# First attention: a unit's transposes and value products one step later, transposes ahead of the scores

## The chip, the core and the metric

The program runs on one core of one Trainium2 chip. The metric is the device time of that core in microseconds (us). The engines are called as the profile calls them: PE is TensorE (matrix products and transposes; PEld is its weight load), ACT is ScalarE, DVE is VectorE, POOL is GpSimd, SP issues most DMAs. Each engine works through a program of its own, in the order in which it is written; semaphores hold it until another engine has come far enough.

## The reference, cut to what matters

Two transformer blocks run one after the other on 512 tokens of width 1024, in float32. The change touches the attention of the first block only:

```
proj  = rmsnorm(x) @ w_in                       # q, k, v of all heads, gates
o_swa = softmax(q.k/8 - slope*dist, window 128, with a sink) @ v      # 8 heads, 2 kv heads
o_cmp = softmax(q.k_cmp/8 - slope*dist) @ v_cmp                       # 8 heads, 31 compressed keys
o_sl, o_win = softmax(q.k/8 - slope*dist, causal) @ v                 # 8 heads each
o_nsa = gate0*o_cmp + gate1*o_sl + gate2*o_win
x     = x + rmsnorm(concat(o_nsa, o_swa) @ w_o)
```

(The selection may keep 16 blocks and there are only 8, so `o_sl` is plain causal attention.) After it come a gated MLP with a convolution, an embedding, and the second block (neighbourhood attention, retention, MLP). None of that is touched.

## The kernel before, in words

**Number format.** Every float32 operand is held as a high part and a low part, and a product of two such operands takes three matmuls (`triple`, lines 593 to 595). ACT makes the high part of a weight piece (line 1323), DVE or, for pieces that come four after a fill piece, POOL makes the low part (lines 2022 and 2943).

**Units.** The first attention is cut into 28 units. Units 0 to 7 are "swa" (one head each, scores in two PSUM banks). Units 8 to 27 are four rounds of five: one "cmp" unit (both kv heads at once, one bank), then "sl", "wn", "sl", "wn" (one head each, three banks). A wide unit u passes through these stages:

1. PE: scores (`scores1`, lines 799 and 800), 8 matmuls.
2. DVE: bias added, row minimum taken, from PSUM to the buffer `pp` in SBUF (`soft1`, line 2191).
3. ACT: exponential and row sum, in place (line 1510).
4. DVE: reciprocal of the four row sums (`norm1`, line 2272). POOL: four multiplications of `pp` by the reciprocal, and by the gate (lines 2969 and 2971). The texts call this the division.
5. PE: transposes (`turn1`, line 813), 7 in a swa unit, 10 in another, into two or three banks. The first transposes of an sl or wn unit already need all four multiplications.
6. ACT: high part of the transposed probabilities (line 1516). DVE: low part, which also frees the banks (`rest1`, line 2207).
7. PE: value products (`values1`, lines 826 and 827), 8 matmuls; cmp units and the second sl unit of a round bring one matmul of line 866.
8. Where the unit closes an output (every swa and every wn unit): ACT copies half of it out (line 1521), DVE adds the other half (`out_add`, line 2214); for every second one ACT and DVE then split the pair (lines 1525 and 2219).

A cmp unit does the same with small tensors and with its division on DVE (lines 2260 to 2266).

**Steps.** All five engines run one loop over steps s, each with its own stages and its own order. In step s PE does: weight matmuls of a fill piece (12 matmuls for a piece; `FILL1`, line 29, says which pieces go into which step: projections, later the output product `w_o_swa`), scores of unit s+1, transposes of unit s-1, value products of unit s-2. DVE does: scaling of a filled product, `soft1(s)`, `out_add(s-3)`, the low part of a pair, reciprocal of s-1, `rest1(s-2)`, low parts of filled queries or keys. ACT does: copies of filled products (line 1533 is that of `w_o_swa`), exponential of s, high part of a weight piece, high part of transposed s-1, output half of s-2, high part of a pair. POOL does: division of s-1, low part of a weight piece.

**PSUM banks.** The eight banks are handed out first in, first out (`Banks`, line 178): who takes a bank waits until the readers of what it held before are done. Banks of scores of unit s and of transposes of unit s-2 are given back at the start of PE's step s.

**Buffers.** `pp` has three buffers, taken in turn by wide units; `soft1(u)` waits for the transposes of the wide unit three before. The transposed probabilities have two; ACT waits for the value products of the wide unit two before.

Of the kernel before, what the change touches and what calls it, by code (L numbers as in the profile page):

```python
# [27 lines left out]

FILL1 = {0: [("w_swa", 6), ("w_swa", 7)], 1: [("w_swa", 8)], 2: [("w_nsa", 0), ("w_swa", 9)], 3: [("w_nsa", 1)],
         4: [("w_nsa", 8)], 5: [("w_nsa", 9)], 6: [("w_nsa", 2)], 8: [("w_nsa", 3)], 9: [("w_nsa", 10)],  # L30
         10: [("w_nsa", 11)], 11: [("w_nsa", 12)], 12: [("w_o_swa", 0), ("w_nsa", 13)],
         14: [("w_o_swa", 1), ("w_o_swa", 2)], 15: [("w_nsa", 14)], 16: [("w_nsa", 15)], 18: [("w_o_swa", 3)],
         21: [("w_o_swa", 4)], 23: [("w_o_swa", 5)], 26: [("w_o_swa", 6)], 27: [("w_o_swa", 7)]}

# [217 lines left out]
def build(nc, ins, out):  # L252
    ctx = ExitStack()
    with ctx:
# [272 lines left out]
        def out_key(u):  # L527

            kind, j, g = unit(u)
            return ("ob", "swa" if kind == "swa" else "nsa", j, g)  # L530

        def closes(u):
            return unit(u)[0] in ("swa", "wn")
# [4 lines left out]
        def out_sum(key):  # L538
            return OS[key[2] % 2]
# [43 lines left out]
        def tensor(e):  # L583
# [188 lines left out]
            def comp_keys():  # L772
                b, free = bank.take(("kc",))
                e.wait_ge(*free, s_fn.at(("hid", 0)))
                t.matmul(b[0:64, 0:62], cw2[0][:, :], chid[0][:, 0:62], start=True, stop=True).then_inc(*s_cm.up("kc"))
                bank.give(("kc",))
# [103 lines left out]
            def give_turned(u):  # L880
                for i in range(1 if unit(u)[0] == "cmp" else 2 if unit(u)[0] == "swa" else 3):
                    bank.give(("tr", u, i))
# [6 lines left out]

            scores1(0)  # L890
            later = []
            for s in range(N_UNITS + 2):
                if s < N_UNITS:
                    give_scores(s)
                if s >= 2:
                    give_turned(s - 2)
                for name, i in FILL1.get(s, ()):
                    key, n = fill_info(name, i)
                    if name == "w_o_swa":
                        part(name, i, B, swa_out, [4, 5, 6, 7], key, True, True)  # L900
                    else:
                        part(name, i, A, x0s, [4 * n, 4 * n + 1, 4 * n + 2, 4 * n + 3], key, n == 0, n == 1,
                             (lambda j, kv=HIDDEN[name, i]: hidden_quarter(kv, j)) if (name, i) in HIDDEN else None)
                    if n == 1:
                        later.append(key)
                if s == 1:
                    comp_keys()
                if s + 1 < N_UNITS:
                    if s + 1 == 8:
                        comp_values()  # L910
                    scores1(s + 1)
                for key in later:
                    bank.give(key)
                later.clear()
                if 1 <= s <= N_UNITS:
                    turn1(s - 1)
                if s >= 2:
                    values1(s - 2)

            def nsa_out(k):  # L920
                return s_xl.at(("ob", "nsa", k))
# [388 lines left out]
        def scalar(e):  # L1310
# [207 lines left out]
            def out_part(key, g, dst, ready, *free):  # L1518

                e.wait_ge(ready, *free)  # L1520
                a.activation(dst[half(g), :], bank.ap(key)[half(1 - g), :], ACT.Copy).then_inc(*s_cp.up(key))
# [16 lines left out]
                    keys_of(key[1], KS1[key[1]])  # L1538

            later = []  # L1540
            for s in range(N_UNITS + 3):
                for name, i in later:
                    filled(name, i)
                if s < N_UNITS:
                    kind, j, g = unit(s)
                    if kind == "cmp":
                        e.wait_ge(s_sf.at(s))
                        for g in range(2):
                            p3 = pc[:, :].rearrange("p (b g n) -> p g b n", b=4, g=2)[:, g, :, 0:31]
                            m = a.activation(p3, p3, ACT.Exp, scale=SLOPES[8 + j + 4 * g])  # L1550
                        m.then_inc(*s_ex.up(s))
                    else:
                        m = expo(SWA if kind == "swa" else NSA, s, probs(s), M4[s % 6], S4[s % 6], s_sf.at(s))
                        if kind == "swa":
                            m = a.activation(G4[s % 6], M4[s % 6], ACT.Exp, bias=sink[:, j + 4 * g:j + 4 * g + 1])
                        m.then_inc(*s_ex.up(s))
                if s == 0:
                    hidden(0)
                    hidden(1)
                if s == 2:  # L1560
                    comp_keys()
                if s == 8:
                    e.wait_ge(s_cm.at("vc"), s_z.at("zero"))
                    for g in range(2):
                        x = slice(32 * g, 32 * g + 31)
                        for r in (0, 64):
                            m = a.activation(VC[g][r + 32 * g:r + 32 * g + 31, half(0)], bank.ap(("vc",))[x, 0:64], ACT.Copy)
                    m.then_inc(*s_qh.up("vc"))
                for name, i in later:
                    behind(name, i)  # L1570
                if 1 <= s <= N_UNITS:
                    u = s - 1
                    kind, j, g = unit(u)
                    if kind == "cmp":
                        e.wait_ge(s_tr.at((u, 0)), *([s_pv.at(u - 2)] if u > 8 else [s_ad.at(("n0", 7))]))
                        a.activation(pct[0:64, :], bank.ap(("tr", u, 0))[0:64, :], ACT.Copy).then_inc(*s_th.up((u, 0)))
                    else:
                        v = unit_back(u, 2)
                        turned(SWA if kind == "swa" else NSA, u, PT[buf_of(u)], [s_pv.at(v)] if v >= 0 else [])
                if s >= 2 and s - 2 < N_UNITS and closes(s - 2):  # L1580
                    key = out_key(s - 2)
                    n = key[2] + (0 if key[1] == "swa" else 4)
                    out_part(key, key[3], out_sum(key), s_pv.at(s - 2),
                             *([s_xl.at(("ob", "swa", n - 2) if n < 6 else ("ob", "nsa", n - 6))] if n >= 2 else []))
                if s >= 3 and closes(s - 3) and unit(s - 3)[2] == 1:
                    pair = out_key(s - 3)[0:3]
                    out_high(pair, out_sum(pair), out_pair(pair), s_xl.at(("x0", 7)) if pair[1] == "swa" else s_cm.at(("hid", 1)))
                later = FILL1.get(s, ())

# [419 lines left out]
        def vector(e):  # L2009
# [288 lines left out]
                        doubled(key, g, tmp.ap(key), T, KS1[key[1]][g])  # L2298

            later = []  # L2300
            for s in range(N_UNITS + 3):
                for name, i in later:
                    behind(name, i)
                for name, i in later:
                    filled(name, i)
                if s < N_UNITS:
                    soft1(s)
                if s >= 3 and closes(s - 3):
                    key = out_key(s - 3)
                    out_add(key, key[3], out_sum(key))  # L2310
                if s >= 4 and closes(s - 4) and unit(s - 4)[2] == 1:
                    pair = out_key(s - 4)[0:3]
                    out_low(pair, out_sum(pair), out_pair(pair))
                if 1 <= s <= N_UNITS:
                    norm1(s - 1)
                if s == 3:

                    g3 = gates[:, :].rearrange("p (b h k) -> p b h k", b=4, h=8)[:, :, :, 0]
                    e.wait_ge(s_fn.at(("gates", 3)))
                    v.tensor_tensor(g3, g3, rowv.unsqueeze(2).broadcast_to([P, 4, 8]), ALU.mult).then_inc(*s_dv.up("gv"))  # L2320
                if s == 8:
                    e.wait_ge(s_qh.at("vc"))
                    for g in range(2):
                        x = slice(32 * g, 32 * g + 31)
                        for r in (0, 64):
                            m = v.tensor_tensor(VC[g][r + 32 * g:r + 32 * g + 31, half(1)], bank.ap(("vc",))[x, 0:64],
                                                VC[g][x, half(0)], ALU.subtract)
                    m.then_inc(*s_ql.up("vc"))
                    bank.read(("vc",), (s_ql, "vc"))
                if 2 <= s <= N_UNITS + 1:  # L2330
                    rest1(s - 2)
                for name, i in later:
                    filled_low(name, i)
                if s == 2:
                    for g in range(2):
                        e.wait_ge(s_z.at("zero"))
                        doubled(("k", "c"), g, tmp.ap(("k", "c")), 31, KC1[g])
                later = FILL1.get(s, ())
# [923 lines left out]
```

## Time and profile before

| | |
|---|---|
| median of three runs | 1309.33 us (1309.13 to 1311.11) |
| profiled execution, own time | 1308.19 us |
| its span (first to last instruction) | 1306.4 us |
| PE busy | 1272.6 us (97%) |
| DVE, ACT, POOL busy | 785.3, 648.5, 222.5 us |
| granted PE clock, mean | 0.994 |

The busy share of PE is close to the whole span; what PE does not use lies almost wholly in the first attention, between about 60 and 250 us. Times in the rows are us from the span's start, means marked in the page are ns. "[0.46 <-POOL pp L2969]" behind a row is idle time of that engine just before the instruction, and the instruction that ended it.

### The profile page before, as it was taken

Reading aid. Unit: us, or ns where it says so; the run is one execution under the profiler, and the core shown is the slowest. Engines: PE = TensorE matmul, PEld = TensorE weight load, DVE = VectorE, ACT = ScalarE, POOL = GpSimd, SP = SyncE. Lnnn points to the kernel's source line nnn. Section 1 sums busy time; section 2 is a strip of 40 time slices with the busy share of each in tenths; the row PEclk is TensorE's granted clock in tenths of the full one; section 3 lists DMA queues with packets and bytes.
Section 4 is the critical chain, followed back from the end, with each engine's and each line's share of the span. In section 5 each row is a group of like instructions: output and inputs, shape, how many; then the busy total and the mean of one; then the engine's idle time right before and its main releaser. Section 6 shows DMA issues by size and latency. Waiting matters only on the chain.

```text
span 1306.4 us, 16459 instructions
## 1 busy us (share of the span) xinstructions
PE 1272.6 (97%) x6004; PEld 1050.4 (80%) x6004; DVE 785.3 (60%) x1465; ACT 648.5 (50%) x1261; POOL 222.5 (17%) x234
## 2 busy tenths in 40 slices
PE   9997998999999999999999999999999999999998
PEld 8876787777888888888878877887888888888887
DVE  5677777486664556345778886589744343344335
ACT  6686767564344443233545655477543242242334
POOL 0065544300110011001002100022311020020111
PEclk9998999999999999999999999999999999999999
DMA  7211110143332333332322221342232323233331
GB/s 266 89 41 33 41 41 25 54 155 97 97 89 89 105 102 92 98 96 85 120 78 89 81 74 49 123 124 78 81 105 91 99 86 105 88 105 89 105 89 66
DMA packets 64625, 118.20 MB, mean 90 GB/s; under 512 B 7712, under 2 KB 12192, under 8 KB 64288
## 3 DMA queue, kind: packets, MB, share of 16 engines
q1 hardware_dynamic: 62704, 112.86, 28.4%
q10 hardware_dynamic: 1840, 4.29, 1.1%
q8 instruction: 48, 0.79, 0.2%
q14 instruction: 33, 0.27, 0.1%
HBM read 115.02 MB, written 2.10 MB: 90 GB/s over the span
## 4 chain that ended last, share of the span: by engine, by line
PE 88%; DVE 5%; POOL 3%; ACT 2%; issue 2%; DMA 1%; POOLq 0%; SPq 0%; DVEq 0%; ACTq 0%
PE bank L593 25%; PE bank L595 24%; PE bank L594 24%; PE bank L813 2%; POOL pp L2969 2%; PE bank L693 2%; PE bank L694 2%; PE bank L695 2%; PE bank L826 1%; PE bank L827 1%; POOL pp L2971 1%; PE bank L799 1%; PE bank L800 1%; PE bank L767 1%; DVE q2p L2191 0%
## 5 line engine op out<-in xcount | busy, mean ns | idle before, releaser
L2022 DVE TENSOR_TENSOR wl<-raw,wh 128x512 fp32r<-128x512 f32 (+2 forms) x360 | 267.9, 755 | 327.4 <-ACT wh L1323 326.7
L1323 ACT ACTIVATE wh<-raw 128x512 fp32r<-128x512 f32 (+1 forms) x398 | 242.2, 619 | 286.2 <-PE bank L595 273.9
L593 PE MATMUL bank<-AH,wh 128*128 128x512 f32 (+1 forms) x848 | 333.4, 393 | 2.1 <-DVE AL L2036 0.8
L595 PE MATMUL bank<-AH,wl 128*128 128x512 f32 (+1 forms) x848 | 328.9, 388 | 0.0
L594 PE MATMUL bank<-AL,wh 128*128 128x512 f32 (+1 forms) x848 | 326.5, 385 | 0.0
L593 PE MATMUL bank<-BH,wh 128*128 128x512 f32 x624 | 248.0, 397 | 0.0
L595 PE MATMUL bank<-BH,wl 128*128 128x512 f32 x624 | 244.9, 393 | 0.0
L594 PE MATMUL bank<-BL,wh 128*128 128x512 f32 x624 | 243.4, 390 | 0.0
L595 PEld LDWEIGHTS bank<-AH,wl 128*128 128x128 f32 x848 | 159.3, 188 | 35.7
L593 PEld LDWEIGHTS bank<-AH,wh 128*128 128x128 f32 x848 | 159.7, 188 | 35.0 <-issue 2.9
L594 PEld LDWEIGHTS bank<-AL,wh 128*128 128x128 f32 x848 | 159.5, 188 | 33.0 <-issue 0.2
L595 PEld LDWEIGHTS bank<-BH,wl 128*128 128x128 f32 x624 | 117.4, 188 | 27.3
L593 PEld LDWEIGHTS bank<-BH,wh 128*128 128x128 f32 x624 | 117.7, 189 | 25.9 <-issue 1.9
L594 PEld LDWEIGHTS bank<-BL,wh 128*128 128x128 f32 x624 | 117.5, 188 | 25.8 <-issue 0.5
L2988 POOL TENSOR_TENSOR BL<-tmp,BH 128x512 fp32r<-128x512 f32 x22 | 28.6, 1298 | 354.5 <-ACT BH L1632 354.5
L3016 POOL TENSOR_TENSOR AL<-tmp,AH 128x512 fp32r<-128x512 f32 x32 | 40.6, 1300 | 269.6 <-ACT AH L1954 269.6
L2943 POOL TENSOR_TENSOR wl<-raw,wh 128x512 fp32r<-128x512 f32 x38 | 50.6, 1335 | 105.9 <-ACT wh L1323 105.9
L813 PE MATMUL bank<-ident,pp 128*128 128x128 f32 x216 | 36.3, 290 | 16.8 <-POOL pp L2971 9.3
L1510 ACT ACTIVATE pp<-pp,small 128x128 f32<-128x128 f32 (+2 forms) x96 | 50.2, 530 | 4.5 <-DVE small L2191 4.2
L1516 ACT ACTIVATE pth<-bank 128x512 fp32r<-128x512 f32 (+1 forms) x64 | 30.2, 530 | 35.6 <-PE bank L813 35.5
L2805 DVE TENSOR_TENSOR X<-X,bank 128x512 f32<-128x512 f32 x46 | 31.5, 687 | 24.3 <-PE bank L595 24.2
L2971 POOL TENSOR_SCALAR pp<-pp,small,gates 128x128 f32<-128x128 f32 (+1 forms) x64 | 39.3, 628 | 39.2 <-DVE small L2272 39.2
(332 smaller groups left out, 1621.2 us busy)
## 6 DMA issues: line engine op xcount, KB each, us to landing
raw<-in_w_dn SPq DMA_DIRECT2D x104, 256.0 KB, 2.7
raw<-in_w_gu SPq DMA_DIRECT2D x88, 256.0 KB, 2.6
raw<-in_w_up SPq DMA_DIRECT2D x64, 256.0 KB, 2.6
raw<-in_w_nsa SPq DMA_DIRECT2D x16, 256.0 KB, 2.7
raw<-in_w_pg SPq DMA_DIRECT2D x16, 256.0 KB, 2.6
raw<-in_w_naq SPq DMA_DIRECT2D x16, 256.0 KB, 2.6
nbi<-in_na_bias ACTq DMA_DIRECT2D x8, 448.0 KB, 3.5
raw<-in_w_swa SPq DMA_DIRECT2D x10, 256.0 KB, 2.7
```

The costliest lines, as they stand in the source:

```text
L593: t.matmul(o, w, xh, start=start, stop=False, skip_group_check=skip)
L594: t.matmul(o, w, xl, start=False, stop=False, skip_group_check=skip)
L595: return t.matmul(o, wl, xh, start=False, stop=stop, skip_group_check=skip)
L813: m = t.transpose(b[:, c:c + P], pp[:, s:s + P], ident[:, :])
L1323: a.activation(W[i % NW].h[:, 0:n], RAW[i % NRAW][:, 0:n], ACT.Copy).then_inc(*s_wh.up(i))
L1510: m = a.activation(o, o, ACT.Exp, bias=m4[:, qb:qb + 1], scale=-1.0, accum_out=s4[:, qb:qb + 1])
L1516: a.activation(pt.h[:, o:o + w], bank.ap(("tr", u, i))[:, 0:w], ACT.Copy).then_inc(*s_th.up((u, i)))
L2022: v.tensor_tensor(w.l[:, 0:n], RAW[i % NRAW][:, 0:n], w.h[:, 0:n], ALU.subtract).then_inc(*s_wl.up(i))
L2805: v.tensor_tensor(chunk(X, c), chunk(X, c), bank.ap(key)[:, :], ALU.add).then_inc(*s_sv.up(done))
L2943: g.tensor_tensor(w.l[:, 0:n], RAW[i % NRAW][:, 0:n], w.h[:, 0:n], ALU.subtract).then_inc(*s_wlg.up(i))
L2971: m = g.tensor_scalar(o, o, r, gate_of(u)[:, qb:qb + 1], ALU.mult, ALU.mult)
L3016: g.tensor_tensor(x.l, tmp.ap(("rs", 8 * gi + k))[:, 0:T], x.h, ALU.subtract).then_inc(*s_xlg.up(("up", 8 * gi + k)))
```

## The change

PE takes the transposes of unit s-2 instead of s-1 in step s, and does them after the fill and ahead of the scores of unit s+1; the value products are those of unit s-3. The loops are one step longer. ACT and DVE follow: high parts of transposed s-2, output half of s-3, pair of s-4; DVE adds output s-4, splits pair s-5, and does `rest1(s-3)` ahead of the reciprocal of s-1 instead of behind it. POOL's program is as before. The fill piece `w_o_swa` 0 goes from step 12 to step 13, which also swaps it with `w_nsa` 13 in the order of the weight pieces.

```diff
@@ FILL1
-         10: [("w_nsa", 11)], 11: [("w_nsa", 12)], 12: [("w_o_swa", 0), ("w_nsa", 13)],
+         10: [("w_nsa", 11)], 11: [("w_nsa", 12)], 12: [("w_nsa", 13)], 13: [("w_o_swa", 0)],
@@ tensor
-            for s in range(N_UNITS + 2):
+            for s in range(N_UNITS + 3):
                 if s < N_UNITS:
                     give_scores(s)
-                if s >= 2:
-                    give_turned(s - 2)
+                if s >= 3:
+                    give_turned(s - 3)
                 for name, i in FILL1.get(s, ()):
...
                 if s == 1:
                     comp_keys()
+                if 2 <= s <= N_UNITS + 1:
+                    turn1(s - 2)
                 if s + 1 < N_UNITS:
                     if s + 1 == 8:
                         comp_values()
                     scores1(s + 1)
                 for key in later:
                     bank.give(key)
                 later.clear()
-                if 1 <= s <= N_UNITS:
-                    turn1(s - 1)
-                if s >= 2:
-                    values1(s - 2)
+                if s >= 3:
+                    values1(s - 3)
@@ scalar
-                if 1 <= s <= N_UNITS:
-                    u = s - 1
+                if 2 <= s <= N_UNITS + 1:
+                    u = s - 2
...
-                if s >= 2 and s - 2 < N_UNITS and closes(s - 2):
-                    key = out_key(s - 2)
+                if 3 <= s < N_UNITS + 3 and closes(s - 3):
+                    key = out_key(s - 3)
...
-                if s >= 3 and closes(s - 3) and unit(s - 3)[2] == 1:
-                    pair = out_key(s - 3)[0:3]
+                if s >= 4 and closes(s - 4) and unit(s - 4)[2] == 1:
+                    pair = out_key(s - 4)[0:3]
@@ vector
                     soft1(s)
-                if s >= 3 and closes(s - 3):
-                    key = out_key(s - 3)
+                if s >= 4 and closes(s - 4):
+                    key = out_key(s - 4)
                     out_add(key, key[3], out_sum(key))
-                if s >= 4 and closes(s - 4) and unit(s - 4)[2] == 1:
-                    pair = out_key(s - 4)[0:3]
+                if s >= 5 and closes(s - 5) and unit(s - 5)[2] == 1:
+                    pair = out_key(s - 5)[0:3]
                     out_low(pair, out_sum(pair), out_pair(pair))
+                if 3 <= s <= N_UNITS + 2:
+                    rest1(s - 3)
                 if 1 <= s <= N_UNITS:
                     norm1(s - 1)
...
-                if 2 <= s <= N_UNITS + 1:
-                    rest1(s - 2)
```

## Rows read from the trace of the kernel before

**Rows 1.** The page's first part: busy time, share of the span, instructions.
```profile
PE 1272.6 (97%) x6004; PEld 1050.4 (80%) x6004; DVE 785.3 (60%) x1465; ACT 648.5 (50%) x1261; POOL 222.5 (17%) x234
```
**Rows 2.** Windows: length, busy PE, PEld, DVE, ACT, POOL, granted clock, DMA share.
```profile
84.00:102.00 18.00, 15.73 (x93) 12.78 (x91) 16.91 (x48) 15.83 (x45) 13.42 (x15) 1.00 0.15 45
...
60.00:250.00 190.00, 169.52 (x974) 144.13 (x974) 131.61 (x391) 132.45 (x365) 98.18 (x120) 0.96 0.13 37
```
**Rows 3.** Waits of PE, 55 to 260 us: total us, times, longest us.
```profile
PE bank L813 <- POOL pp L2971: 9.3, 15, 2.0
PE bank L813 <- POOL pp L2969: 7.1, 15, 1.8
PE bank L799 <- issue: 2.8, 1, 2.8
PE bank L799 <- ACT acc L1533: 0.8, 1, 0.8
```
**Rows 4.** Windows of PE alone: length, busy PE, granted clock, DMA share.
```profile
112.00:120.00 8.00, 5.33 (x19) 0.57 0.19 62
128.00:132.00 4.00, 1.19 (x8) 1.00 0.00 0
200.00:208.00 8.00, 7.27 (x32) 0.79 0.00 0
244.00:252.00 8.00, 7.35 (x34) 0.79 0.18 44
```
**Rows 5.** Chain of waits, 55 to 260 us: start, us, what (one swa step).
```profile
103.94 0.60 ACT os L1521
104.56 0.69 DVE os L2214
105.76 3.51 POOL pp L2969 x4
```
**Rows 6.** Timeline of PE, first instructions of three stages of a swa step.
```profile
89.84 0.44 PE L593 MATMUL bank<-AH,wh 128*128 128x512 f32 x1
...
92.64 0.22 PE L799 MATMUL bank<-ka_s,qs 128*128 128x128 f32 x1
...
93.59 0.49 PE L813 MATMUL bank<-ident,pp 128*128 128x128 f32 x3
```
**Rows 7.** Timeline of PE, first instructions of the stages of a wide step.
```profile
216.49 0.39 PE L799 MATMUL bank<-ka_sl,qs 128*128 128x512 f32 x1
...
217.77 1.36 PE L813 MATMUL bank<-ident,pp 128*128 128x128 f32 x10
218.88 0.48 PE L866 MATMUL bank<-pct,vc 128*128 128x512 f32 x1
219.20 0.40 PE L826 MATMUL bank<-pth,v 128*128 128x512 f32 x1
...
220.48 0.44 PE L799 MATMUL bank<-ka_wn,qs 128*128 128x512 f32 x1
```
**Rows 8.** Groups of DVE, 60 to 250 us: busy us, mean ns, idle before.
```profile
L2207 DVE TENSOR_TENSOR ptl<-bank,pth 128x512 fp32r<-128x512 f32 x40 | 25.7, 675 | 2.4 <-ACT pth L1516 2.2
...
L2214 DVE TENSOR_TENSOR os<-bank,os 64x512 f32<-64x512 f32 x15 | 10.3, 688 | 22.2 <-ACT os L1521 22.2
```
**Rows 9.** Group of ACT, 60 to 250 us, the copy of a filled output product.
```profile
L1533 ACT ACTIVATE acc<-bank 128x512 f32<-128x512 f32 x8 | 4.8, 608 | 0.1
```
**Rows 10.** Timeline of DVE: the last item of step 9, a key's low part.
```profile
130.14 0.69 DVE L2105 TENSOR_TENSOR kb_wn<-tmp,ka_wn 64x512 fp32r<-64x512 f32 x1
```
**Rows 11.** Timeline of POOL: two divisions of sl and wn units.
```profile
141.12 2.81 POOL L2971 TENSOR_SCALAR pp<-pp,small,gates 128x128 f32<-128x128 f32 x4 [2.06 <-DVE small L2272]
...
146.42 2.38 POOL L2971 TENSOR_SCALAR pp<-pp,small,gates 128x128 f32<-128x128 f32 x4 [0.81 <-DVE small L2272]
```
**Rows 12.** Timeline of DVE beside the first of them.
```profile
142.55 1.92 DVE L2109 TENSOR_TENSOR qs<-tmp,qs 64x512 fp32r<-64x512 f32 x2
```
**Rows 13.** Timeline of DVE near the loop's end.
```profile
241.68 0.68 DVE L2214 TENSOR_TENSOR os<-bank,os 64x512 f32<-64x512 f32 x1 [5.70 <-ACT os L1521]
```

More of the change, by code:

```diff
@@ L1540, in scalar @@
             later = []
-            for s in range(N_UNITS + 3):
+            for s in range(N_UNITS + 4):
                 for name, i in later:
@@ L1579, in scalar @@
                         turned(SWA if kind == "swa" else NSA, u, PT[buf_of(u)], [s_pv.at(v)] if v >= 0 else [])
-                if s >= 2 and s - 2 < N_UNITS and closes(s - 2):
-                    key = out_key(s - 2)
+                if 3 <= s < N_UNITS + 3 and closes(s - 3):
+                    key = out_key(s - 3)
                     n = key[2] + (0 if key[1] == "swa" else 4)
-                    out_part(key, key[3], out_sum(key), s_pv.at(s - 2),
+                    out_part(key, key[3], out_sum(key), s_pv.at(s - 3),
                              *([s_xl.at(("ob", "swa", n - 2) if n < 6 else ("ob", "nsa", n - 6))] if n >= 2 else []))
-                if s >= 3 and closes(s - 3) and unit(s - 3)[2] == 1:
-                    pair = out_key(s - 3)[0:3]
+                if s >= 4 and closes(s - 4) and unit(s - 4)[2] == 1:
+                    pair = out_key(s - 4)[0:3]
                     out_high(pair, out_sum(pair), out_pair(pair), s_xl.at(("x0", 7)) if pair[1] == "swa" else s_cm.at(("hid", 1)))
@@ L2300, in vector @@
             later = []
-            for s in range(N_UNITS + 3):
+            for s in range(N_UNITS + 4):
                 for name, i in later:
```

## The prediction

> **What bounds the kernel now.** I read the busy shares first: PE is busy 97% of the span [rows 1], so the only thing to win is PE idle time and PE time at the lower clock. The windows say where: from 60 to 250 us PE is busy 169.5 of 190.0 us, 20.5 us idle [rows 2], against 1306.4 − 1272.6 = 33.8 us in the whole span [rows 1]. The waits of PE name the causes: its transposes wait 9.3 + 7.1 = 16.4 us, 30 times, for the division on POOL; one wait of 2.8 us stands before the scores of unit 10, one of 0.8 us before scores whose bank ACT still reads [rows 3]. The waits do not show the clock. In three windows of 8 us the granted clock is 0.57, 0.79 and 0.79, that is 1.2 GHz for a part of each; what that costs is (1 − clock) × busy: 0.43 × 5.33 + 0.21 × 7.27 + 0.21 × 7.35 = 2.3 + 1.5 + 1.5 = 5.4 us [rows 4]. All that can be won is 20.5 + 5.4 = 25.9 us.
>
> The chain of waits shows why the division is late. It goes round: value products end, ACT copies the output half (0.60), DVE adds the other (0.69), only then comes the reciprocal, POOL divides (3.51), PE transposes and does the next value products [rows 5]. PE itself needs less per step: 12 weight matmuls take 92.64 − 89.84 = 2.8 us, 8 swa scores 0.95 [rows 6], swa value products (8 matmuls of the same widths) as much, 7 transposes 0.8 (seven tenths of the 1.11 us that ten take from 217.77 to 218.88); a wide unit takes 1.28 for scores, 1.11 for transposes, 1.28 for value products [rows 7].
>
> **The change part by part.**
>
> *Transposes and value products a step later.* No PE instruction is added or removed, so PE's busy time at full clock stays. The division of unit s-1 may now end as late as after the fill of step s+1. Take t as the end of value products s-4, the last PE work of step s-1. Where they close an output, DVE's queue from t is: 0.60 for ACT, 0.69 for `out_add` [rows 5], then the moved `rest1` (three times 0.5 to 0.68, some 1.6; two, some 1.2, in swa [rows 8]), then the reciprocal, 0.2: t + 3.1. The division adds 2.4 [rows 11], or 3.5 in swa [rows 5]: t + 5.5 or 6.2. PE reaches the transposes at t + 3.7 without any fill, t + 6.5 with one in either step, t + 9.3 with two. So nearly all of the 16.4 us goes; what stays is in the steps without a fill (7, 17, 19, 20, 22, 24, 25, then 28 and 29). In 17, 19, 22 and 24 a step with a fill or a cmp unit lies in front. POOL's low parts of weight pieces keep their place behind the division and are made four pieces ahead, so they cost nothing; SP's queue is as before, and its loads follow the low parts.
>
> *What comes in its place.* I followed the first-in-first-out order of the banks through all steps.
> - Step 7: reciprocal of 5 stands behind `out_add` 2, a pair's split (0.7), `rest1` 3: t + 3.5, division until t + 7.0; PE has 2.8 + 0.8 + 0.95 + 0.95 = 5.5. 1.5 us, and 0.5 for value products behind `rest1` 4: 2.0.
> - Steps 3 to 6: DVE was busy 16.9 of 18.0 us from 84 to 102, ACT 15.8 [rows 2]. The step shrinks (28 steps in 190 us are 6.8 on average, PE's work in a swa step with a fill is 5.5) and DVE's work does not; bounds 0 and the 1.1 us of idle that DVE has per 18, over four steps 4 us at most. I take 2.0.
> - Step 9: the scores of unit 10 wait for a key's low part, DVE's last item of the step, which ended its first half at 130.8 [rows 10]. Transposes now fill 0.8 of those 2.8 us, and one pair's split (0.7) falls in another step: 1.3 left.
> - Step 14: fill `w_o_swa` 1 takes the bank of `w_o_swa` 0, which came a step earlier, as its first work. It needs ACT's output half of unit 10 (0.60, [rows 5]) and the copy of the fill (0.61, [rows 9]) after t: 1.3 with the handovers. The old 0.8 at the copy goes, since another bank comes there.
> - Steps 19 and 24: the second bank of transposes was the output that `out_add` reads: t + 1.4 against four transposes, 0.5: 0.8 each (with the handovers), 1.6.
> - Steps 20, 25 and 27: 0.2, 0.2 and 0.4, bounds 0 and 1 each.
> - End: value products of 26 need `out_add` 25 and the first part of `rest1` 26: 0.60 + 0.69 + 0.68 = 2.0 against 1.1 of transposes 27; then `rest1` 27 (1.6) against 1.28: 1.2.
>
> Sum: 2.0 + 2.0 + 1.3 + 1.3 + 1.6 + 0.8 + 1.2 = 10.2 us idle in place of 20.5: 10.3 us won. The extra step costs nothing more at the end: the last reciprocal stood behind an `out_add` that had kept DVE idle for 5.70 us [rows 13], and now has no such add in front.
>
> *The clock.* The longest waits for the division, 1.8 and 2.0 us [rows 3], stand at the start of the first and ahead of the last of the three windows. I take it that one of the larger size remains: 5.4 − 2.3 = 3.1 won; the bounds are 0 and 5.4. That a wait of 2.8 us need not bring it is seen at 128 to 132: PE was busy 1.19 of 4.00 us and the clock stayed at 1.00 [rows 4].
> The Trainium skill (TensorE: Matmul & The Clock Gate, "What's actually happening") says that the gate watches recent PE activity in a way that does not start anew with the kernel's work, so that a dip may move from one wait to another. The trace agrees, with the larger wait unpunished. By that rule all dips could stay (1299.0) or all go (1293.6).
>
> *The shared port.* The division of 2.38 us ran 2.81 where DVE's low part of queries, which has two SBUF inputs, ran beside it [rows 11, 12]. That low part now follows the reciprocal at once. It matters only where the division is awaited, in step 7: 0.4 us, inside the 2.0 above.
> The Trainium skill (SBUF — State Buffer, "SBUF: two separate sides") states that GpSimd and a DVE instruction with two SBUF inputs exclude each other for a whole instruction. By it the 1.92 us could be lost whole: 1.5 us more, 1297.4. The trace shows 0.43.
>
> *The swap in the fills.* Step 12 loses 2.8 us of PE work and step 13 gains them; both were without a wait for weights. Zero, bounds ±0.8.
>
> Total: 10.3 + 3.1 = 13.4 us. The profiled execution took 1308.19 us, 1.8 more than its span; the median is 1.1 above it. The saving goes off either: 1309.3 − 13.4 = 1295.9.
>
> **The rivals.**
> *A. DVE and ACT take over as the bound of the swa steps.* For: DVE 94% busy from 84 to 102 [rows 2]. Against: over 60 to 250 us it has 58 us idle, and from 104 on it waits for ACT's halves (22.2 us in all, [rows 8]). Then the 7.1 us of waits for L2969 come back as waits for banks and low parts, and the dip of 2.3 stays: 13.4 − 3.1 − 2.3 = 8.0 won, 1301.3.
> *B. The change doesn't do what it says.* Divisions are still waited for, now because the reciprocal stands behind `rest1`, and bank waits double to 20: within 2.6 us of 1309.3. For: in two steps without a fill one after the other (19, 20) the sum above has no slack. Against: only two such pairs exist.
> *C. Slower.* The moved `rest1` (1.2 or 1.6 us ahead of each of the reciprocals) makes every division late by more than the step covers, so that PE waits in each of 28 steps. It decides from 13.4 / 28 = 0.48 us per step on; at 0.6 us it is 28 × 0.6 = 16.8 against 13.4, 1312.7. For: the chain from t is 5.5 to 6.2 us, longer than a bare step of 3.7. Against: 21 of 28 steps have a fill of 2.8 us.
>
> **How the numbers follow.** My forecast 0.60, with its own range 1291 to 1300; A 0.25; B 0.06; C 0.09. What a measurement can tell from no change is 0.2%, 2.6 us: that is B. Faster 0.85, same 0.06, slower 0.09. Range: below, the best case wins 25.9 − 6 = 20 us (1289.5); above it takes in A with its bounds, 1305.5.
>
> **What would show it.** Right: waits of PE on L2969 and L2971 fall from 16.4 to under 3 us; PE idle between 60 and 240 is near 10 us; new waits of PE on ACT L1521 or L1533 and on DVE L2214 or L2207, under 1.5 us each; the attention's last value products end some 13 us earlier than now, near 237; nothing after that changes but by the shift. Wrong: waits on POOL above 6 us (B or C), DVE idle under 1 us per 18 through all swa steps (A), or a granted clock under 0.9 in new places.

## The result and the profile after

The changed kernel took 1289.9 us (median of 4 runs, 1287.4 to 1291.0), the kernel before 1309.7 beside it: a ratio of 0.9845 (95% interval 0.9828 to 0.9862), 20 us less. A second set gave 1289.1 and 0.9836 (0.9820 to 0.9852). I had forecast 1295.9 with a lower end of 1289.5; by the ratio the time is 1289.0 on the forecast's base of 1309.3, just below that end. The direction and the mechanism held; the gain is half as large again as forecast.

The page after, first part, as in [rows 1]:
```profile
PE 1265.6 (98%) x6004; PEld 1046.8 (81%) x6004; DVE 785.8 (61%) x1465; ACT 648.0 (50%) x1261; POOL 224.9 (17%) x234
```
The same number of PE instructions, and yet PE is busy 7.0 us less. That is the line my sum had no term for. Waits of PE from 55 to 260 us, after (total us, times, longest), against [rows 3]:
```profile
PE bank L813 <- ACT acc L1533: 2.9, 3, 1.3
PE bank L813 <- POOL pp L2969: 1.7, 3, 0.8
PE bank L593 <- ACT acc L1533: 1.6, 2, 1.3
PE bank L799 <- issue: 1.6, 1, 1.6
PE bank L813 <- POOL pp L2971: 0.6, 2, 0.4
PE bank L799 <- DVE os L2214: 0.4, 1, 0.4
PE bank L724 <- DVE r_bc L2086: 0.2, 1, 0.2
```
Waits for the division fall from 16.4 us in 30 to 2.3 us in 5. The most frequent releaser of PE is now, with five waits as well, ACT's copy of a `w_o_swa` product. To compare like with like I take the stretch from the first scores of unit 2 to the last value products, called the loop below. Windows of PE (length, busy, granted clock, DMA share), the kernel before:
```profile
72.25:250.30 178.05, 157.57 (x897) 0.96 0.13 36
```
and after:
```profile
70.69:230.30 159.61, 150.64 (x897) 0.98 0.14 41
...
104.00:112.00 8.00, 7.54 (x30) 0.57 0.20 48
...
200.00:208.00 8.00, 6.70 (x46) 1.00 0.14 37
224.00:232.00 8.00, 7.42 (x44) 1.00 0.32 78
```
The loop is 18.4 us shorter, with the same 897 matmuls. Idle falls from 20.5 to 9.0 us: 11.5. Within the loop the low clock now stands in one place, behind the wait of step 7, and not at the end [rows 4]. With (1 − clock) × busy summed over windows of 8 us from 60 on it costs 3.0 us in place of 5.7: 2.7. The rest is 4.2 us of busy time at equal clock (151.9 against 147.7). Summed over windows of 0.5 us the clock parts are 3.3 and 5.9 us, and the busy time at equal clock is 147.4 against 151.6: the same 4.2. The whole span is 18.4 us shorter too: the profiled execution of before came to the loop 1.6 us later, and that of after had 1.7 us of low clock between 764 and 772 us, where no code differs.

Where most of the 4.2 us sit is seen in the transposes. Timeline of PE, one swa unit before:
```profile
93.59 0.49 PE L813 MATMUL bank<-ident,pp 128*128 128x128 f32 x3
94.39 0.44 PE L813 MATMUL bank<-ident,pp 128*128 128x128 f32 x2 [0.32 <-POOL pp L2969]
95.29 0.44 PE L813 MATMUL bank<-ident,pp 128*128 128x128 f32 x2 [0.46 <-POOL pp L2969]
```
and one after:
```profile
87.30 0.93 PE L813 MATMUL bank<-ident,pp 128*128 128x128 f32 x7
```
Broken by two waits, seven transposes are shown as 0.49 + 0.44 + 0.44 = 1.37 us of busy time; unbroken they are 0.93. That is 0.22 us per wait beside the idle time shown. The ends of matmuls are modelled in the profile, but the starts say the same: from the first transpose to the next stage it is 1.89 us before (93.59 to 95.48) and 0.68 after (87.30 to 87.98), 1.21 us more with 0.78 us of idle time shown. I read it as the end of a matmul that nothing follows to overlap with; that reading is argued, the size is shown. Group of the transposes, 60 to 250 us before (busy us, mean ns, idle before):
```profile
L813 PE MATMUL bank<-ident,pp 128*128 128x128 f32 x216 | 36.3, 290 | 16.8 <-POOL pp L2971 9.3 <-POOL pp L2969 7.1
```
and 60 to 235 us after:
```profile
L813 PE MATMUL bank<-ident,pp 128*128 128x128 f32 x216 | 29.1, 276 | 5.2 <-ACT acc L1533 2.9 <-POOL pp L2969 1.7 <-POOL pp L2971 0.6
```
The same 216 transposes hold 7.2 us less of busy time (a part of it clock) and 11.6 us less of idle.

### The profile page after: what moved, and what is told of

Read it like the earlier page. It is cut to its first block, busy times and chain, and to the rows that moved or that the text cites. A ratio compares the mean times of both kernels' runs of the same rounds, so it can differ in the third digit from the quotient of the medians.

```text
span 1288.0 us, 16448 instructions
## 1 busy us (share of the span) xinstructions
PE 1265.6 (98%) x6004; PEld 1046.8 (81%) x6004; DVE 785.8 (61%) x1465; ACT 648.0 (50%) x1261; POOL 224.9 (17%) x234
## 4 chain that ended last, share of the span: by engine, by line
PE 90%; DVE 5%; issue 1%; ACT 1%; POOL 1%; DMA 1%; POOLq 0%; SPq 0%; DVEq 0%; ACTq 0%
PE bank L593 26%; PE bank L595 25%; PE bank L594 25%; PE bank L813 2%; PE bank L693 2%; PE bank L695 2%; PE bank L694 2%; PE bank L826 1%; PE bank L827 1%; PE bank L799 1%; PE bank L800 1%; DVE pp L2191 1%; PE bank L767 1%; DVE ptl L2207 1%; DVE q2p L2191 0%
## 5 line engine op out<-in xcount | busy, mean ns | idle before, releaser
L595 PEld LDWEIGHTS bank<-AH,wl 128*128 128x128 f32 x848 | 159.5, 188 | 35.4
L594 PEld LDWEIGHTS bank<-AL,wh 128*128 128x128 f32 x848 | 159.6, 188 | 33.0 <-issue 0.2
L2969 POOL TENSOR_SCALAR pp<-pp,small 128x256 f32<-128x256 f32 (+1 forms) x32 | 29.2, 928 | 73.7 <-DVE small L2272 73.7
L2869 DVE SCALAR_TENSOR_TENSOR tmp<-bank,r_bc 128x512 f32<-128x512 f32 x32 | 22.0, 691 | 27.6 <-PE bank L595 16.1
```

The lines of the kernel that those rows point to most:

```text
L594: t.matmul(o, w, xl, start=False, stop=False, skip_group_check=skip)
L595: return t.matmul(o, wl, xh, start=False, stop=stop, skip_group_check=skip)
L2969: m = g.tensor_scalar(o, o, r, None, ALU.mult)
```

## The experiments

Two theories stood at the start. Mine: the extra step hides the division, and a wait costs its idle time, the matmul that ends alone in front of it, and the low clock. The rival: the order inside the step (transposes first, `rest1` first, the swap of the fills) makes the gain. Each group of runs had its own runs of the kernel before; "loop" is the stretch above in the profiled execution.

**One part of the change at a time.** Scores first again, the extra step kept:
```diff
-                if 2 <= s <= N_UNITS + 1:
-                    turn1(s - 2)
                 if s + 1 < N_UNITS:
...
                 later.clear()
+                if 2 <= s <= N_UNITS + 1:
+                    turn1(s - 2)
```


> The changed kernel with the scores of unit s+1 ahead of the transposes of unit s-2 again; the distance of one more step stays. My theory (the distance makes the gain, the order inside the step is worth little): DVE's soft1(u) now waits for transposes of u-3 that come after scores u in the same step, 0.7 to 1.1 us later, which costs only where DVE is short of time: 1290 to 1293 us, waits of PE for the division stay under 3 us. Rival (the order inside the step makes the gain): 1300 us or more, with new waits of PE's transposes or scores of more than 8 us in all.

Measured: 1295.0 us, ratio 0.9892 (0.9877 to 0.9906); loop 166.6. By the ratios (0.9845 and 0.9836 for the change) that is some 6 us more than the change, outside my 1290 to 1293, though far from the rival's 1300; the division is waited for only once, for 0.3 us. The waits of all engines, 66 to 240 us, hold a line that the changed kernel's do not:
```profile
DVE pp L2191 <- PE bank L813: 9.5, 5, 2.8
```
DVE's `soft1` waits for the transposes of the unit three before, and these now come behind its own scores. Its waits for PE are 22.2 us in all here and 17.6 in the changed kernel. PE also waits longer for ACT's copy of a `w_o_swa` product (8.4 us in six waits against 4.5 in five) and for outputs and the compressed values, so the line alone does not show the cause; a run below separates the two. The order inside the step is worth some 6 of the 20 us.

Transposes first alone, without the extra step (in the kernel before):
```diff
+                if 1 <= s <= N_UNITS:
+                    turn1(s - 1)
                 if s + 1 < N_UNITS:
...
                 later.clear()
-                if 1 <= s <= N_UNITS:
-                    turn1(s - 1)
```


> The kernel before with the other half alone: transposes of unit s-1 ahead of the scores of unit s+1, no extra step. My theory: the division is needed 0.95 us (swa) to 1.28 us (wide) earlier than before and comes no sooner, so each of the 24 wide units waits longer by about that: 24 x 1.0 to 1.2 = 24 to 29 us more, 1333 to 1338 us. Rival (the order makes the gain): 1300 us or less.

Measured: 1340.6 us, ratio 1.0246 (1.0231 to 1.0261). Waits for the division:
```profile
PE bank L813 <- POOL pp L2971: 19.6, 32, 2.2
PE bank L813 <- POOL pp L2969: 11.3, 20, 3.0
```
30.9 us in 52 waits. It lost 32 us where 24 to 29 were expected, and by another path: the waits for the division are only 14.5 us longer, 0.6 us for each of 24 wide units and not 1.0 to 1.2, and the low clock (23 us of it in the loop against 5.7) is most of the rest.

DVE's order as before, `rest1` behind the reciprocal:
```diff
-                if 3 <= s <= N_UNITS + 2:
-                    rest1(s - 3)
                 if 1 <= s <= N_UNITS:
                     norm1(s - 1)
...
+                if 3 <= s <= N_UNITS + 2:
+                    rest1(s - 3)
                 for name, i in later:
                     filled_low(name, i)
```


> The changed kernel with DVE's rest1(s-3) behind the reciprocal of s-1 as before the change. My theory: with the extra step either order hides; the reciprocal comes 1.2 us (swa) to 1.6 us (wide) earlier, so that the wait for the division in step 7 (1.7 us in three pieces) goes, and value products get their low parts 0.2 us later: 1288 to 1290 us. Rival (the moved low parts free the banks in time and are a part of the gain): 1293 us or more, with waits of PE on DVE L2207.

Measured: 1290.4 us, ratio 0.9856 (0.9841 to 0.9871). No difference from the changed kernel that can be told; the moved low parts have no part in the gain that can be told. The waits for the division fell from 1.7 to 0.7 us in the swa units, others came, and the loop is 161.4 us.

The fills as before:
```diff
-         10: [("w_nsa", 11)], 11: [("w_nsa", 12)], 12: [("w_nsa", 13)], 13: [("w_o_swa", 0)],
+         10: [("w_nsa", 11)], 11: [("w_nsa", 12)], 12: [("w_o_swa", 0), ("w_nsa", 13)],
```


> The changed kernel with w_o_swa 0 back in step 12. My theory: it needs the pair of units 6 and 7, which DVE splits in that very step behind soft1(12); PE waits 0.3 to 1 us at the step's start and has less work in step 13: 1289 to 1292 us. Rival (the swap is a real part of the gain): 1293 us or more.

Measured: 1288.5 us, ratio 0.9842 (0.9827 to 0.9856). The swap brings nothing either.

**The suspected cost itself.** The division cut to 8 columns per row block, in the kernel before and in the changed one. These two kernels leave most probabilities undivided, so they serve for timing only:
```diff
-                    o, r = pp[:, L["off"][qb]:L["off"][qb] + L["w"][qb]], s4[:, qb:qb + 1]
+                    o, r = pp[:, L["off"][qb]:L["off"][qb] + 8], s4[:, qb:qb + 1]
```


> The kernel before, with a division on POOL that multiplies only 8 columns of each of the four row blocks (the other probabilities stay undivided): the wait for the division is nearly taken away and all else kept. My theory (waits for the division with the drained transposes and the low clock behind them were the whole 25 us that could be won, and the extra step does nothing but hide them): waits on POOL fall from 16.4 to 2 to 5 us and the time to 1287 to 1293 us, about that of the changed kernel. Rival (the new order of transposes, scores and low parts wins by itself): 1298 us or more.

> The changed kernel with the same short division. My theory: only what is left of the waits for it can go, 2.3 us of idle in steps 7 and 28, the transposes that run alone there (0.9 us) and the low clock behind step 7 (3.0 us): 1284 to 1287 us. Rival (POOL's division slows DVE or PE elsewhere through shared resources): 1282 us or less, with shorter DVE instructions of line 2109.

Measured: before 1291.4 us, ratio 0.9854 (0.9839 to 0.9868), with 6.4 us of waits for the division left; after 1286.9, ratio 0.9818 (0.9803 to 0.9832), with none. The waits left in the first are above the 2 to 5 us that I expected. So without the new order, and with most of the division taken away, the kernel before gains 19 us, beside 21 us of the change in the same group. In the changed kernel only 2.2 us are left to gain (1289.1 in the same group), and the low clock behind step 7, which I had expected to go, stayed (2.9 us). Waits for the division are what the kernel before loses, and the changed kernel no longer has them: the extra step hides the division.

**What a wait costs.** The transposes of a unit wait once, for the last division, in the kernel before:
```diff
-                            e.wait_ge(divided.at((u, qb)))
+                            e.wait_ge(divided.at((u, 3 if divided is s_nmg else qb)))
```


> The kernel before, but the transposes of a unit wait once, for the last of the four divisions, and then run unbroken. It asks what a wait costs beside its shown idle time. Theory D: each wait also holds 0.15 to 0.2 us that the profile shows as busy, since the transposes behind it run alone; then from 60 to 250 us busy PE falls by 3 to 5 us and idle rises by 6 to 9 us, and the time is 1311 to 1315 us. Rival (the fall of busy time between the two kernels is all the clock): busy PE at equal clock stays within 1 us, and idle rises by the time lost.

Measured: 1320.8 us, ratio 1.0089 (1.0072 to 1.0106); loop 192.2, idle 32.7. The time went up 12 us, well beyond the expected 2 to 6: idle rose by 12.2 us, and so did the low clock (10.3 us in place of 5.7). But the busy time at full clock fell from 151.9 to 149.2 us with fewer waits. (The waits stood ahead of whole runs of transposes, which then ran unbroken.) Over the runs, busy less (1 − clock) × busy, in us, against the waits for the division in the loop:

| kernel | waits | busy | clock part | busy at full clock | the same, windows of 0.5 us |
|---|---|---|---|---|---|
| changed, short division | 0 | 149.7 | 2.9 | 146.8 | 146.3 |
| changed, first and second profile | 5 | 150.6, 149.5 | 3.0, 1.4 | 147.7, 148.1 | 147.4, 147.8 |
| before, short division | 5 | 152.4 | 4.4 | 148.0 | 147.5 |
| before, one wait | 16 | 159.5 | 10.3 | 149.2 | 146.8 |
| before | 30 | 157.6 | 5.7 | 151.9 | 151.6 |

All run the same matmuls, 897 of them in the kernel before. The rival (all clock) does not hold: busy time at full clock falls by 2.7 us or more. The kernel before with the short division, which has the old order, shows that waits and not the order make it fall. 5.1 us over 30 waits are 0.17 us for each, but that is an average of two kernels and no price per wait: for the one-wait kernel the result depends on the windows (149.2 or 146.8 us), as its clock part is large. Four kernels below with ACT's early copy have 149.4 to 149.9 us by the small windows, with two to six waits for the division, a fifth has 147.7. What one of them adds can be seen.

**Can the rest be had?** Nine us of idle are left. ACT's copy of a `w_o_swa` product in its own step:
```diff
+                for name, i in FILL1.get(s, ()):
+                    if name == "w_o_swa":
+                        filled(name, i)
                 if 3 <= s < N_UNITS + 3 and closes(s - 3):
```
(and no longer at the head of the next step).

> The changed kernel, with ACT copying the product of w_o_swa in the step of its fill, ahead of the output half of unit s-3, in place of in the next step behind it. Five waits of PE on that copy (steps 14, 19, 24, 23 or 26, 27: 1.3 + 1.3 + 1.3 + 0.3 + 0.3 = 4.5 us) should go. My theory: in steps 19 and 24 a wait for the output that out_add reads takes their place at 0.8 us each at most, so 3 to 4.5 us less: 1286 to 1288 us. Rival (the waits only move to the low parts, as DVE and ACT are the bound): 1289 us or more.

Measured: 1289.3 us beside 1289.1 of the changed kernel; loop 159.3, as long as that. The five waits on the copy are gone and these have come, the second in place of 0.6 us in two:
```profile
PE bank L813 <- DVE os L2218: 1.5, 2, 1.0
...
PE bank L813 <- POOL pp L2975: 1.0, 3, 0.4
```
(2218 and 2975 are lines 2214 and 2971, four lines on.) Idle fell from 9.8 to 7.9 us, busy rose by 1.9. A part of that rise stands in step 19. Timeline of PE in the changed kernel:
```profile
180.65 1.31 PE L813 MATMUL bank<-ident,pp 128*128 128x128 f32 x10 [1.30 <-ACT acc L1533]
```
and with the early copy:
```profile
178.63 0.49 PE L813 MATMUL bank<-ident,pp 128*128 128x128 f32 x3
179.35 0.33 PE L813 MATMUL bank<-ident,pp 128*128 128x128 f32 x1 [0.22 <-POOL pp L2975]
180.20 0.88 PE L813 MATMUL bank<-ident,pp 128*128 128x128 f32 x6 [0.52 <-DVE os L2218]
```
One wait ahead of the run became two inside it: 0.56 us less idle, 0.39 us more busy. The rival was right on the time; the waits moved to outputs and to the division, though, and not to the low parts. The repeat beside it:

> The changed kernel once more, beside the others of this group on one chip: 1288 to 1292 us.

Measured: 1289.1 us. The fill `w_nsa` 3 in step 7 in place of 8:
```diff
-         4: [("w_nsa", 8)], 5: [("w_nsa", 9)], 6: [("w_nsa", 2)], 8: [("w_nsa", 3)], 9: [("w_nsa", 10)],
+         4: [("w_nsa", 8)], 5: [("w_nsa", 9)], 6: [("w_nsa", 2)], 7: [("w_nsa", 3)], 9: [("w_nsa", 10)],
```


> The changed kernel with the fill w_nsa 3 in step 7, which had none, in place of step 8. My theory: it covers the wait for the division of unit 5 (1.7 us, with up to 3 us of low clock behind it) and brings the low part of the wn key one step earlier, so that the wait of the scores of unit 10 (1.6 to 2.3 us) goes; the transposes of unit 6 now stand in a step without a fill and may wait up to 1 us: 1284 to 1287 us. Rival (DVE bounds steps 3 to 9 anyway, so waits only move): 1288 us or more.

Measured: 1291.0 us, ratio 0.9854 (0.9837 to 0.9872): nothing won. Waits for the division in the swa units fell from 1.7 to 0.9 us and that of step 9 is gone, and this one has come; timeline of PE:
```profile
114.60 0.79 PE L799 MATMUL bank<-ka_sl,qs 128*128 128x512 f32 x1 [3.59 <-DVE vc L2328]
```
The scores of unit 9 take the bank of the compressed values, which DVE frees last in step 8. In the changed kernel's first profile the low clock of steps 7 and 8 covered that wait wholly, in the second it stood there with 1.8 us. My following of the banks, in the prediction, had passed it over.

Scores first together with the early copy (both edits are shown above):

> The changed kernel with scores ahead of transposes, and ACT's copy of w_o_swa products in the step of the fill. It asks why scores first cost 5 to 6 us. Theory 1 (the other order of taking banks makes PE wait five times for that copy, 8.4 us, in place of 4.5): with the copy early the order costs 0 to 2 us, 1289 to 1291 us. Theory 2 (soft1 of a unit waits for transposes that come after its scores, so DVE's chain gets longer): it still costs 5 us, 1293 to 1296 us.

Measured: 1293.6 us, ratio 0.9882 (0.9868 to 0.9897). Beside the early copy alone (ratio 0.9839) scores first still costs 5.6 us, where it cost some 6 without it; the 1.4 us between the medians of scores first alone and of this run are within the intervals. So the copy's bank explains little of it, and the longer chain through `soft1`, which waits 8.8 us for transposes here, is what is left: theory 2. Three waits on the copy still stood there (3.5 us), so theory 1 isn't excluded for all of it. The early copy, the early key and `rest1` behind, together (three edits shown above):

> A candidate for a better version: the changed kernel with w_nsa 3 in step 7, the early copy of w_o_swa products, and rest1 behind the reciprocal. My theory: the three remove the waits of steps 7 and 9, of steps 14, 19 and 24, and of the last division; each may come back in part on DVE: 1282 to 1286 us. Rival (what is left of the loop is bound by DVE and ACT): 1287 to 1290 us.

Measured: 1289.1 us, ratio 0.9848 (0.9833 to 0.9863), with 4.6 us of wait for the compressed values: the rival again. Then the compressed values early, ahead of ACT's exponential and of DVE's `out_add` in step 8; alone, with copy and key, and with the copy. ACT's stream (the same lines are taken out behind the exponential), then DVE's (taken out behind `norm1`):
```diff
                     filled(name, i)
+                if s == 8:
+                    e.wait_ge(s_cm.at("vc"), s_z.at("zero"))
+                    ...
+                    m.then_inc(*s_qh.up("vc"))
                 if s < N_UNITS:
...
                     soft1(s)
+                if s == 8:
+                    e.wait_ge(s_qh.at("vc"))
+                    ...
+                    bank.read(("vc",), (s_ql, "vc"))
                 if s >= 4 and closes(s - 4):
```

> The changed kernel; in step 8 ACT copies the compressed values ahead of its exponential and DVE makes their low part right behind soft1, ahead of the adding of an output, in place of last in the step. It frees the bank that the scores of unit 9 take 2 us earlier; they waited 1.8 us for it (or a low clock covered that wait). My theory (waits one behind the other in steps 7 to 9 cover each other): that wait goes, and 1 to 2 us of time: 1287 to 1288.5 us. Rival (the chain through DVE in steps 8 and 9 only shifts, up to the key's low part that the scores of unit 10 wait for): 1289 us or more, with the wait of L799 in step 9 longer by what step 8 wins.

> The same with w_nsa 3 in step 7 and the early copy of w_o_swa products. With the key a step early the fill covers step 7, and its low part no longer stands in step 9; alone it had only turned the waits into 3.6 us for the bank of the compressed values. My theory: all three waits of steps 7 to 9 shrink to under 2 us together, 1284 to 1287 us. Rival (DVE has no time left in steps 3 to 9): 1288 us or more, and one wait of 3 us or more stays in steps 7 to 9.

> The early low part of the compressed values and the early copy, fills as in the changed kernel. If the two gains add: 1286 to 1288 us. If the copy's waits only turn into waits for DVE in steps 19 to 25, as they did alone: the time of e13 within 1 us.

Measured: 1289.9, 1289.2 and 1289.9 us, each at a ratio of 0.9849 (0.9833 to 0.9866 at the widest). In all three the rival's case came. Waits of PE in the loop of the last:
```profile
PE bank L799 <- issue: 2.5, 1, 2.5
```
That is step 9, where the changed kernel's second profile has 0.5 us, with 1.8 in step 8: what step 8 won, the key's low part in step 9 gave back. No version beats the changed kernel by what can be told; its loop is 159.6 and 159.3 us in its two profiles, seven of these variants with the extra step and transposes first (the fills, the key, the copy, the values) lie between 158.2 and 160.2, and the low parts behind the reciprocal alone at 161.4.

## Why the prediction was wrong, point by point

*What bounds the kernel, and why.* Right. The short division shows that the waits for it, with what hangs on them, are nearly all of the gain.

*Transposes a step later.* Right: 16.4 us of waits became 2.3 (I had put under 3).

*What comes in its place*, forecast 10.2 us, measured 9.0:

| step | forecast | measured |
|---|---|---|
| 7, division of unit 5 | 2.0 | 1.7 |
| 3 to 6, DVE short | 2.0 | 0.4 |
| 9, key's low part | 1.3 | 1.6 |
| 14, the copy's bank | 1.3 | 1.3 |
| 19 and 24 | 2 × 0.8 on `out_add` | 2 × 1.3 on the copy |
| 20, 25, 27 | 0.8 | 0.6, in 23 and 27 |
| end | 1.2 | 0.6, on the division of unit 27 |

In 19 and 24 I named the second bank of the transposes; the first one, of the fill before, is awaited, behind an output half in ACT's queue as in step 14. The rows measured add up to 8.8 us. At the end the value products did not wait visibly. That the sum comes so near is in part luck: steps 3 to 6 were put 1.6 us too high and steps 19 and 24 1.0 too low, and a wait of step 8 for the compressed values' bank, 1.8 us in the second profile, is not in my list. Rival A had a point: from 84 to 102 us DVE is busy 17.65 us of 18 after (16.91 in [rows 2]), and it did not become the bound of that stretch, where PE is busy 17.43. But it is close enough that no single wait can be taken out with profit.

*The clock.* Forecast 3.1, measured 2.7 and, in the second profile, 4.3. One dip stayed in the loop, behind step 7, as taken.

*The term that was missing.* This is the step that failed: "All that can be won is 20.5 + 5.4 = 25.9 us". I read idle and clock and took busy time at full clock as fixed, as "No PE instruction is added or removed, so PE's busy time at full clock stays" says. It fell by 4.2 us, on average 0.17 us for each of the 25 waits that went. With it the loop's sum is 10.3 + 3.1 + 4.2 = 17.6 against 18.4 measured; idle time gave 1.2 us more than I put, the clock 0.4 us less. The range had the same fault: its lower end, 1289.5, is what is left when 20 of those 25.9 us are won. The row that could have told me stood in the timeline: transposes in twos at 0.44 us, where ten in a run take 1.11.

*The base.* The profiled execution of before was 1.1 to 1.5 us below its medians and that of after 0.1 us. So 18.4 us in the profiles are 19.8 and 21.3 in the medians; the last 1.4 to 3 us I can't place. The loop began between 70.2 and 72.3 us in all profiles but one (73.4), a spread of that size.

*The swap, the shared port.* The swap is zero, as put. The port is as forecast for step 7: the division of unit 5, which is awaited there, took 3.99 us with DVE's low part of queries beside it, and 3.50 before, where that low part came later. Timeline of POOL after, and of DVE beside it:
```profile
100.45 3.99 POOL L2969 TENSOR_SCALAR pp<-pp,small 128x128 f32<-128x128 f32 x4 [0.33 <-DVE small L2272]
```
```profile
100.38 1.47 DVE L2109 TENSOR_TENSOR qs<-tmp,qs 64x512 fp32r<-64x512 f32 x2
```
The 0.49 us are near the 0.4 that the sum has inside its 2.0; the 1.5 us more, the prediction's other case for the port, did not come.

*Rivals B and C.* Neither. The order without the extra step is what is slower: there the scores, 0.95 to 1.28 us, no longer cover the division, which shows as 14.5 us of waits, and the low clock takes more than that.

## What to carry to other kernels

When PE waits in many small pieces, count the pieces as well as their length: here each of the 25 waits that went held on average 0.17 us more than its idle time, and a run of matmuls that is shown in twos and threes is the sign. A stage on a slow engine is best hidden by one more step of distance, and the order inside the step then matters through who waits for the moved work (here most likely DVE's buffer, some 6 us). Once three engines are all close to full in a stretch (here PE 17.43, DVE 17.65 and ACT 16.51 of 18 us), a wait that is taken out comes back at the next one; measure the loop's length, not the wait.

## What the runs showed of the hardware

A short DVE instruction can be held up for the length of a POOL instruction. Timeline of POOL in the changed kernel's second profile, the low part of a weight piece, with two SBUF inputs:
```profile
109.73 1.26 POOL L2943 TENSOR_TENSOR wl<-raw,wh 128x512 fp32r<-128x512 f32 x1
```
and of DVE, an addition of four columns with two SBUF inputs:
```profile
109.96 1.05 DVE L2270 TENSOR_TENSOR small<-small 128x4 f32<-128x4 f32 x1
```
It ended at 111.01, when POOL's had ended at 110.99. In the kernel before that addition took 0.155 us on average, in this profile 0.303.

It goes the other way too. The first of unit 5's four multiplications took 1.09 us in the changed kernel, with DVE's low part of queries begun 0.07 us before it, and 0.60 in the kernel before. Two divisions of `sl` and `wn` units, at 131 and 144 us, also had that DVE line begun 0.07 us before them and took 3.30 us, where others took 2.38.

A multiplication of 8 columns on POOL mostly took 0.30 to 0.35 us (the longest 0.82), so that the short division was still 1.2 to 1.4 us or more for its four parts.

The granted clock also fell where PE had no wait: from 764 to 772 us it was 0.79 in both profiles of the changed kernel, with PE busy 8.00 of 8.00 us, and 1.00 in the kernel before. That is 1.7 us in a place that no code change touches, so one profile can't give the clock part of a small difference.
